# Prompt attention: both halves of the values in one stationary tile, and the query blocks of a head in the order 0, 7, 1, 6, 2, 5, 3, 4

## The reference, cut to what matters

```python
def prompt_attention(q, k, v, pos):
    ...
        s = jnp.einsum('bqhd,bkhd->bhqk', qi, k).astype(jnp.float32) * ATTN_SCALE
        mask = k_chunk[None, :] <= qc[:, None]
        s = jnp.where(mask[None, None], s, NEG)
        p = jax.nn.softmax(s, axis=-1).astype(v.dtype)
        return jnp.einsum('bhqk,bkhd->bqhd', p, v)
```

## Time and profile before

| what | value |
| --- | --- |
| median of three runs | 3441.33 us (3438.16 to 3443.86) |
| span of the profiled execution, first to last instruction | 3437.3 us |
| mean granted TensorE clock over the span | 0.938 of 2.4 GHz |
| PE busy / weight loads | 3101.4 us (90%) / 2744.0 us (80%) |
| DVE / ACT / POOL busy | 1664.0 / 1394.9 / 1170.5 us |
| prompt attention, first to last instruction on a score or output | 453 to 1121 us of the span |

### The profile page before, as it was taken

One profiled execution on the slowest core, in us unless ns is written; L12 is line 12 of the kernel. 1 busy time (PEld: TensorE's weight loads), 2 busy tenths in 40 slices (PEclk: granted clock), 3 DMA queues, 4 the chain that ended last, 5 costly groups with the idle time before them and its releaser, 6 DMA issues. The chain is left out here.

```text
span 3437.3 us, 49771 instructions
## 1 busy us (share of the span) xinstructions
PE 3101.4 (90%) x16732; PEld 2744.0 (80%) x16732; DVE 1664.0 (48%) x2867; ACT 1394.9 (41%) x2953; POOL 1170.5 (34%) x640
## 2 busy tenths in 40 slices
PE   6997969898989685999978999999999999899996
PEld 5776757777778574888868999988999998899996
DVE  3534667676767123444423444445444443644445
ACT  4232466666655223222114433343433343444443
POOL 5242131111110324223215333436433435644444
PEclk9997979999999557999999999999999999999998
DMA  3224521111110305222224121213211212322221
GB/s 119 78 76 90 190 57 29 29 29 29 35 24 8 97 27 175 89 88 83 78 90 148 56 66 61 73 49 139 93 62 61 73 50 93 138 75 73 73 73 54
DMA packets 155375, 260.52 MB, mean 76 GB/s; under 512 B 39392, under 2 KB 86656, under 8 KB 153856
## 3 DMA queue, kind: packets, MB, share of 16 engines
q1 hardware_dynamic: 155232, 258.76, 24.5%
HBM read 202.57 MB, written 56.14 MB: 75 GB/s over the span
## 5 line engine op out<-in xcount | busy, mean ns | idle before, releaser
L1929 POOL TENSOR_TENSOR ff_w_lo<-ff_w_raw,ff_w_hi 128x1024 fp32r<-128x1024 f32 x198 | 517.5, 2639 | 747.5 <-ACT ff_w_hi L2000 747.4
L84 PE MATMUL ff_u<-ff_x_hi,ff_w_hi 128*128 128x384 f32 (+1 forms) x2112 | 693.7, 328 | 49.6 <-POOL ff_w_lo L1929 43.0
L85 PE MATMUL ff_u<-ff_x_hi,ff_w_lo 128*128 128x384 f32 (+1 forms) x2112 | 692.4, 328 | 0.0
L86 PE MATMUL ff_u<-ff_x_lo,ff_w_hi 128*128 128x384 f32 (+1 forms) x2112 | 692.2, 328 | 0.0
L84 PEld LDWEIGHTS ff_u<-ff_x_hi,ff_w_hi 128*128 128x128 f32 x2112 | 401.4, 190 | 52.7 <-POOL ff_w_lo L1929 44.3
L85 PEld LDWEIGHTS ff_u<-ff_x_hi,ff_w_lo 128*128 128x128 f32 x2112 | 401.4, 190 | 1.1
L86 PEld LDWEIGHTS ff_u<-ff_x_lo,ff_w_hi 128*128 128x128 f32 x2112 | 401.3, 190 | 0.0
L2115 DVE SCALAR_TENSOR_TENSOR ff_cv_a<-ff_up_a,ff_taps,ff_cv_a 128x768 f32<-128x768 f32 (+1 forms) x132 | 150.8, 1143 | 412.6 <-ACT ff_cv_a L2049 404.6
L2136 DVE TENSOR_TENSOR ff_y<-ff_y,ff_d 128x512 f32<-128x512 f32 x374 | 239.7, 682 | 146.3 <-PE ff_d L86 146.2
L84 PE MATMUL ff_d<-ff_w_hi,ff_h_hi 128*128 128x512 f32 x748 | 292.4, 391 | 11.9 <-DVE ff_y L2136 11.9
L85 PE MATMUL ff_d<-ff_w_hi,ff_h_lo 128*128 128x512 f32 x748 | 292.2, 391 | 0.0
(11 more groups left out here) (341 smaller groups left out, 6384.5 us busy)
## 6 DMA issues: line engine op xcount, KB each, us to landing
ff_w_raw<-in_w_ffn_p SPq DMA_DIRECT2D x198, 512.0 KB, 3.5
pj_raw<-in_x_t SPq DMA_DIRECT2D x40, 256.0 KB, 3.0
mx_work<-in_w_mix_p SPq DMA_DIRECT2D x18, 512.0 KB, 4.5
mx_m_raw<-scratch_mix_t SPq DMA_DIRECT2D x17, 512.0 KB, 5.3
mx_x_raw<-in_x SPq DMA_DIRECT2D x17, 512.0 KB, 4.3
scratch_x_t<-mx_work SPq DMA_DIRECT2D x17, 512.0 KB, 3.2
scratch_y<-mx_work SPq DMA_DIRECT2D x17, 512.0 KB, 3.0
ff_y<-scratch_y SPq DMA_DIRECT2D x17, 512.0 KB, 6.8
```

The lines of the kernel that those rows point to most:

```text
L84: pe.matmul(out, lh, rh, start=first, stop=False, **kw)
L85: pe.matmul(out, ll, rh, start=False, stop=False, **kw)
L86: return pe.matmul(out, lh, rl, start=False, stop=last, **kw)
L1929: pool.tensor_tensor(w_lo[:, slot], w_raw[:, n % RAWS, :].rearrange("p (k c) -> p k c", c=P), f32(w_hi[:, slot]), ALU.subtract).then_inc(w ...
```

## The change

1. The stationary operand of the values is one tile of 128 columns, v_hi beside v_lo. Each key tile takes two matmuls (pt_hi and pt_lo as moving operand) where it took three. Rows 0 to 63 of the output bank hold v_hi's part, rows 64 to 127 v_lo's part (which now also has the lo*lo term). ACT copies the lower part out (low_row) instead of the reciprocals; DVE adds the two parts (whole) and then multiplies by the reciprocals, straight from PSUM: one more DVE operation and one more wait (joined) for each pair.
2. The eight pairs of a head are taken in the order 0, 7, 1, 6, 2, 5, 3, 4, so that the tiles of a head come as 0, 1, 14, 15, 2, 3, 12, 13, 4, 5, 10, 11, 6, 7, 8, 9. The pieces of the next head are split in another order, the scores wait accordingly, and the stores go to the block's place.
3. The scale of the scores is put on q in `phase_heads` (a scale of the ACT copy, and a three-operand DVE operation in place of a two-operand one), so that the bias operation goes, in `phase_attend` and in `phase_sample`; the exponential takes the negated maximum.

```diff
@@ phase_heads
-                rows = NOPE if n < 8 else P
-                act.activation(out[0:rows, n % 4, 0:width], ps[n % 8][0:rows, 0:width], ACT.Copy)\
+                rows, by = (NOPE, SCALE) if n < 8 else (P, 1.0)
+                act.activation(out[0:rows, n % 4, 0:width], ps[n % 8][0:rows, 0:width], ACT.Copy, scale=by)\
...
-                    dve.tensor_tensor(rot[64:96, 0, 0:width], ps[n][64:96, 0:width], trig[64:96, 0:width],
-                                      ALU.mult).then_inc(turned, 1)
+                    dve.scalar_tensor_tensor(rot[64:96, 0, 0:width], ps[n][64:96, 0:width], SCALE,
+                                             trig[64:96, 0:width], ALU.mult, ALU.mult).then_inc(turned, 1)
...
@@ phase_attend
-NCH = [t % QT // 4 + 1 for t in range(TILES)]
+PAIR_ORDER = (0, 7, 1, 6, 2, 5, 3, 4)
+ROW = [2 * PAIR_ORDER[t % QT // 2] + t % 2 for t in range(TILES)]
+NCH = [ROW[t] // 4 + 1 for t in range(TILES)]
...
-    n = 2 * (j % 8) + 2
+    n = 2 * PAIR_ORDER[j % 8] + 2
...
-PIECES = (("k", 0), ("q", 0), ("v", 0), ("k", 1), ("q", 1), ("k", 2), ("q", 2), ("k", 3), ("q", 3))
+PIECES = (("k", 0), ("q", 0), ("v", 0), ("q", 3), ("k", 1), ("k", 2), ("k", 3), ("q", 1), ("q", 2))
...
-        v_hi, v_lo = sb("v_hi", [P, 2, QT, VD], F32R), sb("v_lo", [P, 2, QT, VD], F32R)
+        v_pair = sb("v_pair", [P, 2, QT, 2, VD], F32R)
...
-                                           bias=bias[:, e % 2:e % 2 + 1], scale=SCALE,
+                                           bias=neg_all[:, e % 2:e % 2 + 1],
...
-                            act.activation(rec_row[:, :], ps_o[j % 2][0:VD, QB:2 * QB], ACT.Copy).then_inc(rowed, 1)
+                            act.activation(low_row[:, :], ps_o[j % 2][VD:P, 0:QB], ACT.Copy).then_inc(rowed, 1)
...
             def finish(it, j):
                 dve.wait_ge(rowed, nth(it, 16, j))
+                dve.tensor_tensor(whole[:, :], ps_o[j % 2][0:VD, 0:QB], low_row[:, :], ALU.add).then_inc(joined, 1)
+                dve.wait_ge(joined, nth(it, 16, j))
                 dve.wait_ge(stored[j % 2], nth(it, 8, j // 2 - 1) * 16)
-                dve.tensor_tensor(out[:, j % 2, :], ps_o[j % 2][0:VD, 0:QB], rec_row[:, :], ALU.mult)\
+                dve.tensor_tensor(out[:, j % 2, :], ps_o[j % 2][0:VD, QB:2 * QB], whole[:, :], ALU.mult)\
                    .then_inc(normed, 1)
...
-                            dve.wait_ge(biased, nth(it, TILES, k - 1))
+                            dve.wait_ge(expd, nth(it, BASE[TILES], BASE[k - 1] - 1 if k >= 2 else
+                                                  [-1 - NCH[TILES - 1], -1][k]))
                             dve.tensor_reduce(neg_all[:, k % 2:k % 2 + 1], neg_max[:, k % 2, 0:NCH[k]], AX.X, ALU.min)\
                                .then_inc(max_of, 1)
-                            dve.wait_ge(max_of, nth(it, TILES, k))
-
-                            dve.wait_ge(expd, nth(it, BASE[TILES], BASE[k - 1] - 1 if k >= 2 else
-                                                  [-1 - NCH[TILES - 1], -1][k]))
-                            dve.tensor_scalar(bias[:, k % 2:k % 2 + 1], neg_all[:, k % 2:k % 2 + 1], SCALE, None,
-                                              ALU.mult).then_inc(biased, 1)
...
-                    mm = product(pe, ps_o[j % 2][0:VD, cols], (v_hi[:, u, kt, :], v_lo[:, u, kt, :]),
-                                 (pt_hi[:, j % 2, kt, cols], pt_lo[:, j % 2, kt, cols]), kt == 0, kt == last,
-                                 skip_group_check=True)
+                    both = v_pair[:, u, kt].rearrange("p a d -> p (a d)")
+                    pe.matmul(ps_o[j % 2][:, cols], both, pt_hi[:, j % 2, kt, cols], start=kt == 0, stop=False,
+                              skip_group_check=True)
+                    mm = pe.matmul(ps_o[j % 2][:, cols], both, pt_lo[:, j % 2, kt, cols], start=False,
+                                   stop=kt == last, skip_group_check=True)
...
@@ phase_sample
-                    act.activation(prob[:, u, a:b], src[:, 0:b - a], ACT.Exp, bias=stat[:, u, 3:4], scale=SCALE)\
-                       .then_inc(expd, 1)
+                    act.activation(prob[:, u, a:b], src[:, 0:b - a], ACT.Exp, bias=stat[:, u, 2:3]).then_inc(expd, 1)
...
-                dve.tensor_scalar(stat[:, u, 3:4], stat[:, u, 2:3], SCALE, None, ALU.mult).then_inc(biased, 1)
```

More of the change, by code:

```diff
@@ L805, in phase_attend @@
         rec = sb("rec", [P, 4])
-        rec_row = sb("rec_row", [VD, QB])
+        low_row = sb("low_row", [VD, QB])
+        whole = sb("whole", [VD, QB])
         out = sb("out", [VD, 2, QB])
@@ L810, in phase_attend @@
         neg_all = sb("neg_all", [P, 2])
-        bias = sb("bias", [P, 2])
         ps_s = [bank(f"s{i}") for i in range(SBANKS)]
@@ L823, in phase_attend @@
         max_of = sem("max_of")
-        biased = sem("biased")
         expd = sem("expd")
@@ L830, in phase_attend @@
         rowed = sem("rowed")
+        joined = sem("joined")
         normed = sem("normed")
@@ L840, in width @@
         def width(t, c):
-            return CW if c < NCH[t] - 1 else (t % 4 + 1) * P
+            return CW if c < NCH[t] - 1 else (ROW[t] % 4 + 1) * P
         @block.sync
@@ L866, in head @@
                     sp.wait_ge(normed, nth(it, 16, j))
-                    sp.dma_start(g["mix_t"][ds((2 * it + u) * VD, VD), jj * QB:(jj + 1) * QB],
-                                 out[:, j % 2, :]).then_inc(stored[j % 2], 16)
+                    cols = slice(PAIR_ORDER[jj] * QB, (PAIR_ORDER[jj] + 1) * QB)
+                    sp.dma_start(g["mix_t"][ds((2 * it + u) * VD, VD), cols], out[:, j % 2, :])\
+                      .then_inc(stored[j % 2], 16)
             with sp.Fori(0, PAIRS - 1) as it:
@@ L959, in _ @@
         def _(dve):
-            for s, n in ((masked, TILES), (reduced, BASE[TILES]), (max_of, TILES), (biased, TILES),
-                         (ptlo, BASE[TILES]), (totalled, TILES), (recd, TILES), (normed, 16)):
+            for s, n in ((masked, TILES), (reduced, BASE[TILES]), (max_of, TILES),
+                         (ptlo, BASE[TILES]), (totalled, TILES), (recd, TILES), (joined, 16), (normed, 16)):
                 dve.sem_inc(s, n)
@@ L1033, in scores @@
             def scores(it, t, c):
-                u, i = t // QT, t % QT
+                u, i = t // QT, ROW[t]
                 n, w = BASE[t] + c, width(t, c)
-                if i % 4 == 0:
+                if t % 2 == 0 and PAIR_ORDER[t % QT // 2] in (0, 7, 2, 5):
                     s = max(PIECES.index(("k", c)), PIECES.index(("q", i // 4)))
@@ L1053, in values @@
             def values(it, j, key_tiles):
-                u, last = j // 8, 2 * (j % 8) + 1
+                u, last = j // 8, 2 * PAIR_ORDER[j % 8] + 1
                 if 0 in key_tiles:
@@ L1130, in phase_sample @@
         new_turned, nhi, nlo = sem("new_turned"), sem("nhi"), sem("nlo")
-        scored, maxed, least, biased = sem("scored"), sem("maxed"), sem("least"), sem("biased")
+        scored, maxed, least = sem("scored"), sem("maxed"), sem("least")
         expd, summed, recd, normed = sem("expd"), sem("summed"), sem("recd"), sem("normed")
@@ L1222, in exps @@
             def exps(row, u):
-                act.wait_ge(biased, at(row, 1, 0))
+                act.wait_ge(least, at(row, 1, 0))
                 act.wait_ge(turned, at(row - 2, 1, 0))
                 for i, (src, a, b) in enumerate(((ps_s, 0, PAST), (ps_sn, PAST, KEYS))):
-                    act.activation(prob[:, u, a:b], src[:, 0:b - a], ACT.Exp, bias=stat[:, u, 3:4], scale=SCALE)\
-                       .then_inc(expd, 1)
+                    act.activation(prob[:, u, a:b], src[:, 0:b - a], ACT.Exp, bias=stat[:, u, 2:3]).then_inc(expd, 1)
             def step(row, u, fill, ahead=2):
@@ L1267, in _ @@
         def _(dve):
-            for s, n in ((vlo, 1), (nlo, 1), (maxed, 2), (least, 1), (biased, 1), (summed, 1), (recd, 1),
+            for s, n in ((vlo, 1), (nlo, 1), (maxed, 2), (least, 1), (summed, 1), (recd, 1),
                          (normed, 1), (tlo, 2), (llo, 1)):
@@ L1284, in maxima @@
                 dve.wait_ge(maxed, at(row, 2, 1))
-                dve.wait_ge(biased, at(row - 2, 1, 0))
+                dve.wait_ge(expd, at(row - 2, 2, 1))
                 dve.tensor_reduce(stat[:, u, 2:3], stat[:, u, 0:2], AX.X, ALU.min).then_inc(least, 1)
-                dve.wait_ge(least, at(row, 1, 0))
-                dve.wait_ge(expd, at(row - 2, 2, 1))
-                dve.tensor_scalar(stat[:, u, 3:4], stat[:, u, 2:3], SCALE, None, ALU.mult).then_inc(biased, 1)
             def normalise(row, u):
```

8 lines of the change are left out of this document (4 added, 4 removed).

## The result

| what | before | after |
| --- | --- | --- |
| median of four runs | 3441.34 us (3438.16 to 3443.86) | 3483.74 us (3479.28 to 3487.35) |
| ratio, 95% interval | 1 | 1.0126 [1.0114, 1.0138] |
| span of the profiled execution | 3437.3 us | 3481.6 us |
| mean granted clock | 0.938 | 0.935 |
| prompt attention, first score to last output | 667.9 us | 719.8 us |

The kernel is 42.4 us slower, 1.3%; 3481 was predicted. The attention alone lost 51.9 us.

A forecast was written before the change was run, and what follows sets the result against it. No engine is full; a chain through three in-order engines sets the pace. (171.1 walk + 2 + 5 clock - 167.5) x 4 = +42, sample -1.5, heads 0: +40 on 3441.3, about 3481 us; bounds 3420 to 3525.

The forecast's parts named there:

- the walk: Attention chain followed tile by tile in the new order: an iteration sums to 171.1 us before clock costs, ±5.
- falls of the clock within it: New short pairs leave PE little work: five new falls to half clock an iteration, at 1.0 us each.
- Part 1's gain on PE: Values in two matmuls: 7.9 us a head of PE array time, 63 in all, if PE were the bound throughout.
- long pairs under 11: Attention: a long pair under 11 us, or a short one under 8.3, would show the prediction wrong.
- The signs: Attention trace: iterations of 173 to 178 us, more pt_lo waits, value matmuls 0.12 apart, more half-clock stretches behind short pairs.
- The end of an iteration: Last minimum to next iteration: 14.5 us where 19.9 stood, through shorter last values and an earlier last tile, -5.2.
- `finish` on the chain: Added DVE operation in `finish` delays pt_lo and the transposes behind it: 0.5 us each pair.
- The clock: Iteration start at half clock, now over tile 14's scores: 2 us, bounds 0 and 4; plus new falls later.
- Rival B: Attention: the clock falls in every short pair, 1.7 us each for 28: 3509 us, up to 3530; chance 0.14.
- The small terms: Sample phase: eight bias waits gone, 1.5 us won; `phase_heads`: 0, bounded by -1 and +3 us.
- The lower end of its range: Whole kernel: 3420 us, lower bound from the walk's ±5 an iteration and the clock's bounds.
- A half-wide last key tile: Last key tiles of the values: 64 would cost about 0.1 us each instead of winning, under 5 us, left out.

The follow-up runs named there:

- order_only: The kernel before with the alternating order of the pairs alone, values in three matmuls and bias operation kept: 3518.7 us, ratio 1.0224.
- order_scale: The changed kernel with the values back in three matmuls of 64 columns, alternating order and scale on q kept: 3491.3 us, ratio 1.0146.
- finish_last: The changed kernel with both operations of `finish` issued after the step's last slot instead of in its second: 3461.0 us, ratio 1.0051.
- down_after_two: The changed kernel with pair order 0, 1, 7, 6, 5, 4, 3, 2, `finish` after the last slot and the load one store earlier: 3412.1 us, ratio 0.9922.
- load_early: The changed kernel with the load of K, Q and V of the head after next issued one store earlier: 3477.2 us, ratio 1.0110.
- scale_only: The kernel before with the scale on q and no bias operation alone, natural order, values in three matmuls: 3424.6 us, ratio 0.9945.
- load_late: The changed kernel with the load of K, Q and V of the head after next issued one store later: 3496.2 us, ratio 1.0154.
- nat_load_fin: The changed kernel with pairs in natural order, `finish` after the last slot and the load one store earlier: 3404.9 us, ratio 0.9890.

## Why the prediction came out right, point by point

The terms of the walk against the second iteration, between minima (the prediction's own bounds of the groups):

| from tile to tile | walk | measured |
| --- | --- | --- |
| 0 to 3 | 11.3 + 2 clock | 14.7 |
| 3 to 7, 7 to 11, 11 to 15 | 22.3, 21.0, 19.1 | 21.6, 21.0, 19.8 |
| 15 to 16 | 2.9 | 3.2 |
| 16 to 19 | 16.8 | 17.5 |
| 19 to 23, 23 to 27, 27 to 31 | 23.1, 21.0, 19.1 | 23.1, 21.9, 19.8 |
| 31 to 0 | 14.5 | 18.6 |
| falls of the clock within it | 5 | in the rows above |
| sum | 178.1 | 181.0 |

**The walk through the groups** held to 1 us in each, and with it the main reason for the loss: the order costs more than the other parts can win. Part by part it is less good. As the expectation for `order_only` puts the walk in figures, the order was to cost 94 us, part 3 to win 24 and part 1 to win 32. Measured are 77, 27 and at most 8 (nothing in the attention). Part 1's gain on PE was the misjudged step, the order was priced 17 too high, and the two errors largely cancel in the sum. Nor did the walk hold inside a group. The first exponentials of the tiles 19, 21 and 23, in ACT's timeline of the changed kernel:

```profile
736.75 0.69 ACT L940 ACTIVATE at_p<-at_s,at_neg_all 128x512 f32<-128x512 f32 x1
...
748.16 0.68 ACT L940 ACTIVATE at_p<-at_s,at_neg_all 128x512 f32<-128x512 f32 x1
...
759.80 0.69 ACT L940 ACTIVATE at_p<-at_s,at_neg_all 128x512 f32<-128x512 f32 x1
```

The short pair takes 11.4 us and the long one 11.6, where the walk has 9.2 and 13.9. In the four couples of the second head the short pairs take 10.6 on average (walk 9.0) and the long ones 10.7 (walk 11.7). The prediction named long pairs under 11 as a sign that it is wrong, and on average that sign is there; inside the group only the sum was right. `order_scale` shows a part of the cause: with three value matmuls its short pairs take 9.4 and its long ones 11.7, so it is part 1 that puts 1.2 us into a short pair, where its operation was priced at 0.5, and takes 1.0 out of a long one. With `finish` last the short pairs take 9.5 again (`finish_last`), so that what they lost is `finish` on their chain. That the walk charged the long values to the long pair as if nothing covered them fits `down_after_two`, where a long pair with few values is no shorter, but is not shown by itself.

**The signs.** Grown waits for pt_lo, value matmuls 0.12 apart, the second operation of `finish` and exponentials 0.2 after the minimum are there. Iterations of 173 to 178 are not: they took 181 to 183, by the turn and, in the first, by a slower start.

**The end of an iteration** is the term that was mis-sized: 14.5 predicted (by its own figures, 19.9 - 5.2, it is 14.7), 18.3 to 18.6 measured, 11.6 us over three turns. The walk of the drain itself was right: from the last minimum to the reciprocals' matmuls it is 9.4 us (620.54 to 629.93), 14.7 before (770.57 to 785.25), -5.3 for a predicted -5.2; and `load_early`, where nothing is in the way, has 14.8. What was missed is that a drain that gets shorter brings the jump under a load that is tied to the last pairs.

**`finish` on the chain**: 0.5 a pair was the price. Undone for the changed kernel it gives 0.35 a pair for both operations by the medians, 0.44 by the attention, and most of it in the short pairs. In the natural order the same added operation costs more (35.8 - 13.6 = 22.2, 0.35 for the second operation alone), and there it eats all that part 3 wins.

**The clock.** The start was priced at 2 us (bounds 0 and 4). Tile 0 to tile 3 took 14.7 in the second and third iteration, 3.4 above the walk, and 15.9 in the first, 4.6 above it. Inside an iteration five new falls were predicted; the second iteration has three in all: one at 648.9, still in the slow start (0.51 until 652.3), and two at 720.6 and 765.0, both in a short pair of the second head. A fall costs 0.7 to 0.8 where the same group stands with and without it (7 to 11: 21.03 in the second iteration, 21.80 in the first), near the 1.0 taken. By the mean clock (0.93 of 727 us, and 0.96 of 674 before) some 100 us were at half instead of some 54, but much of it over PE that had little to do. Rival B, a fall in every short pair, did not happen. The row before the one at 720.6 has PE busy for 1.11 of 3.40 us; the rule of the Trainium skill ("TensorE: Matmul & The Clock Gate", "HAM oscillation") describes what the trace has here, but in two short pairs of eight, not in all.

**The small terms.** The sample phase was to win 1.5 and its stretch is 5.5 shorter. The wait there is 4.6 shorter than in the earlier trace rows, in the changed kernel's view of waits:

```profile
ACT sa_prob L1228 <- DVE sa_stat L1287: 44.0, 8, 6.6
```

But this is not shown to come from the operation taken out. Among the kernels that have the changed sample code the stretch takes 152.7 to 161.1 us; in `scale_only` it is 160.9 with a wait of 48.4, no better than before. So not even the 1.5 is visible, and the 5.5 is a variation whose cause is open. Heads: the attention begins 1.4 us later, inside the bounds for 0. The feed-forward phase is 3.3 shorter with the same code; it varies by 4 us from kernel to kernel here. So the span's +44.3 is +51.9 (attention), +1.4 (heads), -5.5 (sample), -3.3 (feed-forward), within 0.2, where the prediction has +42 and -1.5. The attention was 10 us worse than forecast, about as much as the turns cost, and the two later stretches 7 us better, by nothing that the prediction knew of: a good part of the closeness of 3481 to 3483.7 is luck. The lower end of its range doesn't come out of its own terms either: the walk's -20 with no cost of the clock gives 3434 and not 3420.

**A half-wide last key tile.** The prediction left out an estimate from the Trainium skill ("TensorE: Matmul & The Clock Gate", "LDWEIGHTS (loading the stationary operand)"), of about 0.1 us for each (64 of them are 6.4 us, where it says under 5). The two half-wide matmuls take 0.27 with the restart behind them (629.66 to 629.93), where the three before took 0.26 (784.99 to 785.25 in the timeline of before). So the last key tile won nothing, as that estimate has it, but not between the two matmuls: they start 0.06 apart (629.66, 629.72), as those with 64 columns do (784.99, 785.04), so no load of 0.107, as the estimate has it, stands between them. What got longer is the restart behind them, 0.21 (629.72 to 629.93) for 0.15 (785.10 to 785.25).

## What to carry to other kernels

In a pipeline through in-order engines where none is full, taking a third of the matmuls off the busiest one is worth almost nothing, and one 0.4 us operation for each pair put in front of what the next engine waits for can cost more than that wins (20 us here, in the natural order): place it behind the row minimum, the exponential's release, before looking for array time to save. Big tiles between small ones did not even out this chain, where each tile's second half falls into its neighbour's steps; compare pair by pair which engines work at once. Issue prefetches so that they land before a loop jumps back, and look again when the end of the loop's body gets shorter. And compare the stretch that was changed, beside the whole: here a phase that the edits leave alone varies by more than some edits are worth.

## What the runs showed of the hardware that was not expected

- A jump back of the loop stands behind a running data load. PE idles 1.4 to 2.1 us at the turn where no load is in the way (1.84 before, 1.96 in `load_early`, 1.49 in `load_late`), 6.63 where 1.75 MB went out 3.3 us before the last matmuls, 5.32 with 1.25 MB; with the load 1.0 us behind PE's last matmuls it is DVE that idles, 8.25 us. Without a load in the way DVE's own jump takes longer than PE's, 2.6 to 2.9 us (`load_early`, `nat_load_fin`). The DMA view of the changed kernel has no instruction packet for 3.7 us of the load (630.5 to 634.2). That the engines wait for such packets is inferred from this and from how the gap moved with the load, since the profile names no releaser.
- ACT loads its table again (1.28 us) at the first exponential of the first three iterations (456.4, 639.2 and 820.2 in the changed kernel), between the minimum and the exponential; in the second and third only copies stand between it and the last exponential. Before and after are alike. The fourth, whose ACT code stands behind the loop, has none, and its exponential starts 0.18 after the minimum instead of 1.62.
- A 128-column stationary tile costs no more than one of 64 between matmuls that use it: 256-wide ones are 0.12 apart and 128-wide ones 0.06 with either. It costs where another operand follows: the transposes start 0.18 after a 256-wide value matmul instead of 0.12 (medians).
